# Norms from per-token sums, lower parts on GpSimd, taps and rows moved: a two-layer hybrid block in FP32 precision

## The reference, cut to what matters

```python
for l in range(DEPTH):
    h = rmsnorm(x, norm_mix[l])
    proj = h @ w_in[l]
    ua, cq, ckv, kr, qc, kc, vc, ud = jnp.split(proj, IN_SPLITS, axis=-1)
    ya = conformer_conv(ua, ...)        # gate, 31-tap causal conv, layernorm, silu, 256x256
    yb = mla(cq, ckv, kr, ...)          # rmsnorm of cq and ckv, rope, 4 causal heads
    yc = diff_attention(qc, kc, vc, ...)# a0 - lam * a1 of two softmaxes, rmsnorm over 64
    yd = multiscale_pool(ud, ...)       # windows of 2, 4, 8, 16 less the value, 64x64 blocks
    x = x + jnp.concatenate([ya, yb, yc, yd], axis=-1) @ w_out[l]
    x = x + memory_cross_attention(rmsnorm(x, norm_xa[l]), mem, ...)
    x = x + conv_glu_ffn(rmsnorm(x, norm_ffn[l]), ffn_up[l], ffn_dw[l], ffn_dw_b[l], ffn_down[l])
return rmsnorm(x, norm_final)
```

## Time and profile before

| | |
|---|---|
| time, median of 3 runs | 1739.59 us (1737.55 to 1739.62) |
| profiled execution, its own time | 1737.64 us |
| its span | 1735.8 us, 21837 instructions |
| TensorE busy | 1613.4 us, 93% |
| VectorE busy | 1125.3 us, 65% |
| ScalarE busy | 700.0 us, 40% |
| GpSimd busy | 263.1 us, 15% |
| mean granted TensorE clock | 0.975 of full |
| read from HBM | 144.97 MB, 88 GB/s with the writes |

### The profile page before, as it was taken

One profiled execution on the slowest core, in us unless ns is written; L12 is line 12 of the kernel. 1 busy time (PEld: TensorE's weight loads), 2 busy tenths in 40 slices (PEclk: granted clock), 3 DMA queues, 4 the chain that ended last, 5 costly groups with the idle time before them and its releaser, 6 DMA issues. The chain is left out here.

```text
span 1735.8 us, 21837 instructions
## 1 busy us (share of the span) xinstructions
PE 1613.4 (93%) x7472; PEld 1239.5 (71%) x7472; DVE 1125.3 (65%) x1600; ACT 700.0 (40%) x1074; POOL 263.1 (15%) x176
## 2 busy tenths in 40 slices
PE   6889889889999999999988998899999999999996
PEld 3467576568767888888876666557867788888874
DVE  8968896664446764764765978665444674575575
ACT  3232355663344432432443244764243442342343
POOL 5513142112011000000020513212102000000002
PEclk9989999899999999999998999999999999999998
DMA  3142123223212333333224212322312232322323
GB/s 136 47 155 86 49 86 104 79 74 97 73 37 85 97 97 98 97 97 96 93 79 143 82 42 85 104 90 73 97 37 73 85 97 97 97 97 90 96 81 109
DMA packets 46205, 153.37 MB, mean 88 GB/s; under 512 B 5808, under 2 KB 6064, under 8 KB 45232
## 3 DMA queue, kind: packets, MB, share of 16 engines
q1 hardware_dynamic: 46128, 152.34, 27.5%
HBM read 144.97 MB, written 7.34 MB: 88 GB/s over the span
## 5 line engine op out<-in xcount | busy, mean ns | idle before, releaser
L688 ACT ACTIVATE wh<-raw 128x1024 fp32r<-128x1024 f32 x246 | 260.3, 1059 | 647.9 <-PE psum L1238 647.8
L1236 PE MATMUL psum<-a_hi,wh 128*128 128x512 f32 x1072 | 426.2, 398 | 12.2 <-DVE wl L927 11.8
L1237 PE MATMUL psum<-a_lo,wh 128*128 128x512 f32 x1072 | 420.4, 392 | 0.0
L1238 PE MATMUL psum<-a_hi,wl 128*128 128x512 f32 x1072 | 420.2, 392 | 0.0
L927 DVE TENSOR_TENSOR wl<-raw,wh 128x1024 fp32r<-128x1024 f32 x210 | 261.5, 1246 | 140.9 <-ACT wh L688 140.9
L1236 PE MATMUL psum<-b_hi,wh 128*128 128x512 f32 x608 | 240.2, 395 | 10.5 <-DVE wl L927 6.1
L1236 PEld LDWEIGHTS psum<-a_hi,wh 128*128 128x128 f32 x1072 | 203.1, 189 | 62.7 <-DVE wl L927 16.6
L1238 PE MATMUL psum<-b_hi,wl 128*128 128x512 f32 x608 | 236.7, 389 | 0.0
L1237 PE MATMUL psum<-b_lo,wh 128*128 128x512 f32 x608 | 236.7, 389 | 0.0
L1237 PEld LDWEIGHTS psum<-a_lo,wh 128*128 128x128 f32 x1072 | 203.2, 190 | 45.0 <-issue 2.9
L1238 PEld LDWEIGHTS psum<-a_hi,wl 128*128 128x128 f32 x1072 | 203.2, 190 | 42.7
(11 more groups left out here) (213 smaller groups left out, 2139.5 us busy)
## 6 DMA issues: line engine op xcount, KB each, us to landing
raw<-in_w_main SPq DMA_DIRECT2D x106, 512.0 KB, 3.5
raw<-in_w_up SPq DMA_DIRECT2D x88, 512.0 KB, 3.5
raw<-in_w_down SPq DMA_DIRECT2D x32, 512.0 KB, 3.5
raw<-in_w_last SPq DMA_DIRECT2D x16, 384.0 KB, 2.9
bias_scratch<-stage SPq DMA_DIRECT2D x64, 64.0 KB, 1.6
bias<-bias_scratch SPq DMA_DIRECT2D x16, 256.0 KB, 4.4
raw<-in_w_first SPq DMA_DIRECT2D x6, 512.0 KB, 3.5
sw<-in_small SPq DMA_DIRECT2D x2, 1152.0 KB, 6.7
```

Of the source, the lines that this page charges most:

```text
L688: act.activation(wh[:, b].rearrange("p k m -> p (k m)")[:, 0:width], raw[:, b, 0:width], ACT.Copy).then_inc(w_hi, 1)
L1236: pe.matmul(out_ap, wh[:, b, k, :], his[:, k, :], start=(begin and i == 0), stop=False)
L1237: pe.matmul(out_ap, wh[:, b, k, :], los[:, k, :], start=False, stop=False)
L1238: last = pe.matmul(out_ap, wl[:, b, k, :], his[:, k, :], start=False, stop=(end and i == len(tiles) - 1))
```

## The change

**Norms.** `product` with ones is replaced by `sums_of`: the squares are the stationary operand, block by block of 128 tokens, and one column of ones moves, so that the sum of token p of block j stands on partition p in column j. ScalarE takes the root of four columns (eight for the sub-norms, which have two halves of 64 features), VectorE the reciprocal of them in `thin`, and `row_of` on TensorE spreads them over all partitions again: four products of a broadcast column with the identity (for the sub-norms eight of 64 rows). For mix, xa and ffn ScalarE copies this row from PSUM into `rbc`; the others are read from PSUM.

**Lower and upper parts.** GpSimd makes the lower parts of chunks 2 to 32 and the upper parts of 25 to 32. Its pooling windows are put behind the lower parts of chunks 10 to 13. Their buffers are moved, and one wait for them is added on ScalarE.

**Row scaling.** In steps 1 to 16 ScalarE scales the exponentials by the inverse row sums (`scale_rows`).

**Taps.** Three behind chunks 2 and 3, five behind 4 to 8, two behind 9, five behind 10 and 11, three behind each `qm`, the last seven at steps 0 and 1.

**What follows them.** `ln_mean` goes from step 11 to 3, `ln_var` from 15 to 7 with its row at 9, Silu from 21 to 11, `pw` from 23 and 25 to 15 and 17, pool from 1 and 3 to 5 and 11, vc from 6 and 8 to 13 and 14, sub0 from 30 to 29 with its row at 31; the w_out tiles change their order (pw before the second latent one).

```diff
-POOL_LO = range(N_WK, N_OUT + 2)
+POOL_LO = range(2, N_OUT + 2)
+POOL_HI = range(25, N_OUT + 2)
...
-                    for i in range(2):
-                        window_sums(i)
-                        window_differences(i)
                     for n in POOL_LO:
+                        if n in POOL_HI:
+                            upper(n)
                         lower(n)
+                        if n in (10, 12):
+                            window_sums(n // 2 - 5)
+                        if n in (11, 13):
+                            window_differences(n // 2 - 5)
...
+                    def upper(n):
+
+                        pool.wait_ge(w_load[n % 2], loads(n, n % 2))
+                        pool.wait_ge(g_full, n - 1)
+                        pool.wait_ge(w_hi, n)
+                        pool.tensor_copy(wh[:, n % 2].rearrange("p k m -> p (k m)"), raw[:, n % 2, :]).then_inc(w_hi, 1)
...
+                    def roots(name, eps, scale, cols=4):
+
+                        act.activation(thin[:, ROOTS.index(name), 0:cols], v_wait(name)[:, 0:cols], ACT.Sqrt, bias=eps,
+                                       scale=scale).then_inc(root, 1)
+
+                    def row_of(name):
+
+                        act.activation(rbc[:], v_wait(f"{name}_row"), ACT.Copy).then_inc(v_act, 1)
...
+                    def scale_rows(m):
+
+                        act.wait_ge(rec_in, m + 1)
+                        e = ering[:, m % RING, :]
+                        act.activation(e, e, ACT.Copy, scale=rec[:, m:m + 1]).then_inc(scaled_in, 1)
...
+                    def inverse(name, cols=4):
+
+                        r = ROOTS.index(name)
+                        dve.wait_ge(root, r + 1)
+                        dve.reciprocal(thin[:, r, 0:cols], thin[:, r, 0:cols]).then_inc(root_inv, 1)
...
                         scaled(n, places[n])
-                        lo(n + 2)
...
                         if n == 8:
-                            latents(0)
-                            latents(1)
-                        if n >= 3:
-                            convolve({8: 0, 9: 2, 11: 4}.get(n, 3))
+                            inverse("stat_q")
+                            inverse("stat_kv")
+                        if n == 9:
+                            latents()
+                        if n >= 2:
+                            convolve({2: 3, 3: 3, 9: 2}.get(n, 5))
 
                     for h in range(4):
                         dve.tensor_tensor(qm(h), v_wait(f"uq{h}"), rope[:], ALU.mult).then_inc(v_dve, 1)
-                        convolve(2)
+                        convolve(3)
...
                         if t < 2:
                             convolve(4)
-                        elif t > 2:
-                            convolve(3)
...
+                    def sums_of(name, *pairs):
+
+                        ps, w = bank(name), pairs[0][1].shape[1]
+                        for j in range(4):
+                            for i, (src, one) in enumerate(pairs):
+                                last = pe.matmul(ps[:, w * j:w * j + w], src[:, P * j:P * j + P], one, start=(i == 0),
+                                                 stop=(i == len(pairs) - 1))
+                        last.then_inc(v_full, 1)
+
+                    def row_of(name, w=1):
+
+                        r = ROOTS.index(name)
+                        ps = bank(f"{name}_row")
+                        pe.wait_ge(root_inv, r + 1)
+                        for j in range(4):
+                            for i in range(w):
+                                inv = thin[:, r, w * j + i:w * j + i + 1].broadcast_to([P, P // w])
+                                last = pe.matmul(ps[P // w * i:P // w * (i + 1), P * j:P * j + P], inv, ident,
+                                                 start=True, stop=True)
+                        last.then_inc(v_full, 1)
+
+                    one = ones[:, 0:1]
+                    sums_of("stat_mix", (ssum, one))
                     gemm(0, 0, a_hi, a_lo)
+                    row_of("stat_mix")
                     gemm(1, 1, a_hi, a_lo)
```

More of the change, by code:

```diff
@@ L79 @@
 SW_UQ0, SW_UQ1, SW_K, SW_V, SW_PW, SW_POOL, NSW = 0, 512, 1024, 1280, 1536, 2048, 2304
-V_USES = ([("stat_mix", "root"), ("stat_q", "root"), ("stat_kv", "root"), ("kr", "act"), ("uq0", "dve"),
+V_USES = ([("stat_mix", "root"), ("stat_mix_row", "act"), ("stat_q", "root"), ("stat_kv", "root"),
+           ("stat_q_row", "dve"), ("stat_kv_row", "dve"), ("kr", "act"), ("uq0", "dve"),
            ("uq1", "dve"), ("uq2", "dve"), ("uq3", "dve")] + [(f"kn{h}", "act") for h in range(4)] +
[L85 to L91, removed]
+          [("vm0", "act"), ("vm1", "act"), ("ln_mean", "dve"), ("pool0", "dve"), ("ln_var", "root"),
+           ("ln_var_row", "dve"), ("pool1", "dve"), ("mla0", "dve"), ("vc0", "act"), ("vc1", "act"),
+           ("pw0", "dve"), ("pw1", "dve"), ("vx0", "act"), ("mla1", "dve"), ("vx1", "act"), ("diff0", "act"),
+           ("vx2", "act"), ("sub0", "root"), ("sub0_row", "dve"), ("diff1", "act"), ("vx3", "act"),
+           ("sub1", "root"), ("sub1_row", "dve"), ("stat_xa", "root"), ("stat_xa_row", "act")] +
+          [(f"xo{i}", "dve") for i in range(8)] + [("stat_ffn", "root"), ("stat_ffn_row", "act")])
+Y_ORDER = {6: "pool0", 7: "pool1", 2: "mla0", 0: "pw0", 1: "pw1", 3: "mla1", 4: "diff0", 5: "diff1"}
 Y_TILES = list(Y_ORDER)
@@ L705, in _ @@
                     hi(1)
[L706 removed]
+                    roots("stat_mix", c("eps6"), 1.0 / D)
+                    row_of("stat_mix")
                     hi(2)
@@ L844, in _ @@
                     hi(N_WQ + 2)
-                    act.activation(rtmp[:], v_wait("stat_xa"), ACT.Sqrt, bias=c("eps6"), scale=1.0 / D).then_inc(root, 1)
+                    roots("stat_xa", c("eps6"), 1.0 / D)
+                    row_of("stat_xa")
                     for n in range(N_WQ + 1, N_WO):
@@ L1418, in norm_sum @@
                         pe.wait_ge(ss_in, n)
-                        product(name, (ones, ssum[:]))
+                        sums_of(name, (ssum, one))
                     gemm(N_WQ, 1, a_hi, a_lo, free="wq", ready=lambda i: pe.wait_ge(x_lo, i + 1))
                     norm_sum("stat_xa", KT)
-                    gemm(N_WQ + 1, 0, a_hi, a_lo, free="wq")
+                    gemm(N_WQ + 1, 0, a_hi, a_lo, free="wq", tiles=range(4), end=False)
+                    row_of("stat_xa")
+                    gemm(N_WQ + 1, 0, a_hi, a_lo, tiles=range(4, KT), begin=False)
                     gemms(N_WQ, KT, a_hi, a_lo, S, "wq", lead=2)
@@ L1466, in _ @@
                             norm_sum("stat_ffn", 2 * KT)
-                            gemm(base + 1, 0, a_hi, a_lo, free="up")
+                            gemm(base + 1, 0, a_hi, a_lo, free="up", tiles=range(4), end=False)
+                            row_of("stat_ffn")
+                            gemm(base + 1, 0, a_hi, a_lo, tiles=range(4, KT), begin=False)
                         gemms(base, 2 * tiles, a_hi, a_lo, S, "up", lead=2 * int(g == 0))
```

202 lines of the change are left out of this document (104 added, 98 removed).

## The result

The changed kernel takes **1760.36 us** (median of 4 runs, 1757.49 to 1761.85), the kernel before 1739.61 beside it (1737.55 to 1740.39): ratio 1.0119, 95% interval 1.0102 to 1.0137, so slower by 20.8 us. The prediction was 1753, in 1721 to 1772. The profiled execution took 1757.49 us, its span 1755.6.

A forecast was written before the change was run, and what follows sets the result against it. TensorE, busy 93% of the span, was taken as the bound. Per layer 19 - 10.5 + 0.9 - 2.9 = +6.5 us, +13 in all, on the median 1739.6 gave 1752.6, forecast as 1753, range 1721 to 1772.

The forecast's parts named there:

- the mixer takes over 175 us: Sign in the mixer's steps: a duration above 175 us would show the forecast wrong.
- VectorE behind through the hold: Projections: taps and GpSimd subtractions exclude each other; held time 27.8 us, so VectorE ends the fourth query product at 212.8.
- Projections +19: Projections, per layer: late query products and TensorE's half clock make the steps begin later, +19 us together.
- The 3 us for the clock: Projections: about 6 us of key and value products at half rate after TensorE's gaps cost 3 us.
- Mixer -10.5: Mixer's steps, per layer: most waits and slow clock of 27 us go, row products cost 3.3; 10.5 us gained.
- clock 1.0: Mixer's steps: loss to slow clock still booked after the change, 1.0 us per layer.
- Sums "no change": Norms: eight weight loads for one-column products cost 0.4 to 1.5 us, taken as no change from the 0.9 before.
- Cross attention +0.9 and FFN -2.9: Per layer: cross attention's row adds 0.9 us; the FFN loses its 2.2 gap and 1.7 of clock, gaining 2.9.
- Row scaling on ScalarE: Mixer's steps: 0.58 us beside 2.9 per step against TensorE's 4.2, not a bound except at table loads.
- Rival A: Projections: the lock stays harmless, taps slip through or slack absorbs the backlog; -9.5 us per layer, 1721; 25%.
- Rival C: Mixer: ScalarE's table stops at steps 7 and 11 block TensorE; gain 2 instead of 10.5, +15 per layer, 1770; 15%.
- The 1760 that the prediction worked out by the rule to the letter: Projections: if GpSimd's tensor_scalars also held VectorE about 1 us each, +4 us per layer, time 1760.

The follow-up runs named there:

- e1: Changed kernel with lower parts 2 to 14 back on VectorE and the pooling windows at their old place: 1744.43 us.
- e2: Changed kernel with GpSimd's lower parts of chunks 2 to 14 covering only 128 of 1024 columns: 1747.15 us.
- e5: e4_both with chunk 12's GEMM moved from step 0 to between the second and third query product: 1724.78 us.
- the fillers: Changed kernel with eight unused matmuls added on TensorE between the second and third query product: 1757.56 us.
- e4_both: Changed kernel with lower parts 2 to 14 back on VectorE and sums made with 128 columns of ones: 1736.07 us.
- e3: Changed kernel with per-token sums made with 128 columns of ones (64 and 64 for the sub-norms): 1751.13 us.
- f1: e5 with the scaling of the 16 first rows back on VectorE: 1734.27 us.
- b1_gpsimd_alone: Kernel before with only lower parts 2 to 14 moved to GpSimd, windows behind those of 10 to 13: 1749.8 us.
- g1_lower_gpsimd_between: e5 with lower parts 2 to 14 on GpSimd again and the windows behind 10 to 13: 1737.87 us.
- the two single parts: Kernel before with only lower parts 2 to 14 on GpSimd (1749.8 us, projections +4.2), and with only the taps early (1738.2 us, projections +6.1).

## Why the prediction was right

The time fell in the range, and on the side forecast with 64%. The mechanism forecast for the projections is the one found, with its size too large. For the mixer the prediction was wrong by its own sign: "the mixer takes over 175 us" stood there as one of being wrong, and it took 178.8.

- **VectorE behind through the hold: right.** Two-layer tap time is 141.0 us against 120 x 0.752 (their median) = 90.2: 25.4 us per layer held, forecast 27.8; 5.3 of it were there before. The fourth query product was scaled at 208.55, forecast 212.8. GpSimd's lower parts cost 15.9 us (e1) and 13.2 (e2) of the 20.8 by experiment, and 13.1 on top of e5.
- **Projections +19: mis-sized, measured +12.55.** 4.3 us of the difference is VectorE's end, as above. The 3 us for the clock were added wrongly: the stretch is there (17.1 us at 0.50, longer than the 3.4 to 10.2 of the earlier trace rows), but by the fillers and the rows behind them nearly all of it was hidden under VectorE's pace. A term on TensorE was added to a term on VectorE, where the later of the two counts.
- **Mixer -10.5: the step that failed, measured -1.92.** Its idle terms were right in sum, partly by luck: kept and new waits forecast at 7.3 and 4.9, so 12.2; the trace has 12.6. The wait before the pair at step 9 came as forecast (1.2), but those at vc1 and pw1, 2.3 and 1.2, were 0.3 and 0.4, and waits for vx (1.3), thin (0.6) and the pooling product (0.5) make up for them. Row products were 1.05 us where 1.1 was taken. What failed is the term "clock 1.0": half-clock time is 20.5 us, not about 2; TensorE is busy for 20.0 of them and loses half, 10.0 us where 1.0 was booked; 8.6 are missing. The prediction took the stretches away together with the waits of 2.6 to 3.8 us ahead of them, and others stood where no wait ahead of them was over 1.3 us. The waits that stay do not fix how many: with nearly the same waits half-clock time per mixer is 20.5 us in the kernel after, 23.9 and 6.8 in e1, 13.7 in e5 and 3.4 in e4_both, where the mixer is -8.9. Neither do the sums: thin ones stand in e1's second layer, wide ones in e5. What sets it stays open.
- **Sums "no change": wrong.** Their duration was about as taken (0.95 to 1.05 for eight records, 2.45 for the sixteen of the q latent), but the clock was at half behind them at 165.06, and wide sums there kept it at 1.00; the prediction had no term for it. The projections were no shorter for it in the first layer and 0.7 us in the second; the 9.2 us of e3 are nearly all in the mixers.
- **Cross attention +0.9 and FFN -2.9: mis-sized.** The gap of the earlier trace rows is gone and no wait stands from 545 to 580 us; yet the third stage grew 0.77, with a half-clock stretch at 393.8 behind the same 1.8 us wait as before, and with the rest of the layer 0.15 us came back, not 2.0.
- **Row scaling on ScalarE: right that it is no bound**; on VectorE it makes e5 9.5 us slower (f1). Upper parts at nothing: right.
- **Rival A** (the lock harmless, 1721) is refuted by b1_gpsimd_alone and g1_lower_gpsimd_between. **Rival C** (steps that don't give back) was forecast by table stops on ScalarE; its sum, mixer -2, is what was measured, from another cause. Per layer the parts are 12.55 - 1.92 - 0.15 = +10.5, forecast +6.5. That the median lies so near the forecast is in part luck, by errors of opposite sign: the projections were forecast 6.5 us too long, the mixer 8.6 and what follows 1.9 too short.

The Trainium skill, "SBUF — State Buffer", section "SBUF: two separate sides", has the hold as an exclusive lock between a VectorE operation with two SBUF inputs and a GpSimd operation that reads SBUF. The tap at 173.58 (2.94 us beside 2.39) agrees; the tap at 180.44, done at 181.49 inside a TENSOR_SCALAR that ran until 181.80, again does not. The 1760 that the prediction worked out by the rule to the letter is the measured time, but not for its reason: it needed longer projections than +19, and they were +12.55.

What stays open: why the same mixer is at 0.93 in one layer and 0.98 in the other; how much of e3's 9.2 us the wide sums make and how much is where the half-clock stretches happened to fall; what the new norms cost or gain by themselves; and what makes the 2 us by which the two single parts (+10.4) fall short of +12.55.

## What to carry to other kernels

Before work goes to GpSimd, look at what VectorE does in those microseconds: a multiply-add from SBUF to SBUF beside a GpSimd tensor_tensor can cost VectorE most of the GpSimd operation's length (2.94 us for a tap of 0.75). Over all 26 lower parts the taps took 41.5 us more than in e1, 1.6 each, windows included, where the offload saves 1.23. When an engine that isn't TensorE paces a stretch, neither a faster clock nor filler helps there; put due work into the wait (11.3 us here). And do not book the half clock behind a removed wait as won: here mixers with nearly the same waits spent 3.4 to 23.9 us at it. Compare two layers of the same code before you put a small gain down to an edit.

## What the runs showed of the hardware that was not expected

- FP32 products with one moving column count as busy in the trace (0.95 to 1.05 us for eight records), but the clock was 0.50 behind them (165.06) and 1.00 with 128 columns in the same place.
- With waits of 1.38, 1.19 and 1.52 us the clock stayed at 1.00 until 205.9 and then fell to 0.51 for 6.8 us; behind one wait of 3.00 it was 0.50 for 10.2 us, with one of 8.40 for 17.1.
- Two layers of one execution differed by 6.8 us in the same instructions, at clocks of 0.93 and 0.98, with the same waits.
